# Loading the odd-numbered weight slabs of a two-block transformer kernel from GpSimd's queue instead of SyncE's

## The reference

```
first block, 2 layers:
  h = h + retention_mixer(rmsnorm(h), ...)                  # layer 0
  h = h + swiglu(rmsnorm(h), gate, up, down)                # dense, 2816 wide
  h = h + per_layer_embedding(h, ...)
  h = h + band_attention_mixer(rmsnorm(h), ...)             # layer 1
  h = h + sum over 8 experts e of gates[e] * swiglu(xn, w_gate[e], w_up[e], w_down[e])   # 3584 wide
  h = h + per_layer_embedding(h, ...)
second block, 2 layers:
  x = x + hybrid_mixer(rms_norm(x), ...)                    # stick-breaking, sparse and gated linear attention
  x = x + square(relu(rms_norm(x) @ w_up)) @ w_down         # 4096 wide
```

## Time and profile before

| | us |
|---|---|
| median of 3 runs (2742.73 to 2752.49) | 2751.07 |
| the profiled execution | 2758.43 |
| its span, from the first instruction to the last | 2756.6 |
| TensorE busy in it | 2576.8 (93%) |
| VectorE busy | 1884.1 (68%) |
| ScalarE busy | 1461.9 (53%) |
| GpSimd busy | 0.2 |

### The profile page before, as it was taken

One profiled execution on the slowest core, in us unless ns is written; L12 is line 12 of the kernel. 1 busy time (PEld: TensorE's weight loads), 2 busy tenths in 40 slices (PEclk: granted clock), 3 DMA queues, 4 the chain that ended last, 5 costly groups with the idle time before them and its releaser, 6 DMA issues.

```text
span 2756.6 us, 32701 instructions
## 1 busy us (share of the span) xinstructions
PE 2576.8 (93%) x13559; PEld 2172.2 (79%) x13559; DVE 1884.1 (68%) x1960; ACT 1461.9 (53%) x1347; POOL 0.2 (0%) x4
## 2 busy tenths in 40 slices
PE   7989999896999999999999989799989999998999
PEld 7858897865788888888888777588758988876898
DVE  7454545545788888888888787557675556767554
ACT  3434334443666766767676666455544335555442
POOL 0000000000000000000000000000000000000000
PEclk9999999967999999999999999899989999998999
DMA  7534764415899999989899977255224554522453
GB/s 225 177 107 157 208 191 160 138 61 198 302 352 343 352 342 323 368 327 370 322 370 325 359 262 269 67 157 174 77 92 155 197 170 151 171 86 88 157 187 134
DMA packets 301812, 597.59 MB, mean 217 GB/s; under 512 B 13552, under 2 KB 105952, under 8 KB 301664
## 3 DMA queue, kind: packets, MB, share of 16 engines
q1 hardware_dynamic: 301664, 595.50, 62.7%
HBM read 594.41 MB, written 1.05 MB: 216 GB/s over the span
## 4 chain that ended last, share of the span: by engine, by line
PE 83%; DVE 11%; ACT 4%; issue 2%; DMA 1%; SPq 0%; DVEq 0%; ACTq 0%
PE ps L211 81%; DVE ring_rounded L702 2%; ACT high_rounded L689 1%; DVE arena_rounded L1884 1%; PE ps L1632 1%; PE ps L1207 1%; DMA ring<-in_w_down_dense 1%; DVE arena L2369 0%; DVE h L852 0%; DVE ring_rounded L1884 0%; DVE xT L639 0%; DVE xT_rounded L645 0%; DVE arena L2499 0%; DVE arena_rounded L712 0%; ACT high_rounded L1687 0%
## 5 line engine op out<-in xcount | busy, mean ns | idle before, releaser
L211 PE MATMUL ps<-high_rounded,arena_rounded 128*128 128x512 f32 x2664 | 838.0, 396 | 24.5 <-DVE arena_rounded L712 12.4
L702 DVE TENSOR_TENSOR ring_rounded<-ring,high_rounded 128x2048 fp32r<-128x2048 f32 (+3 forms) x231 | 513.5, 2231 | 328.3 <-ACT high_rounded L689 327.3
L689 ACT ACTIVATE high_rounded<-ring 128x2048 fp32r<-128x2048 f32 (+3 forms) x231 | 430.2, 1864 | 401.0 <-PE ps L211 386.6
L211 PEld LDWEIGHTS ps<-high_rounded,arena_rounded 128*128 128x128 f32 x2664 | 500.9, 191 | 130.5 <-DVE arena_rounded L712 14.3
L211 PE MATMUL ps<-ring_rounded,arena_rounded 128*128 128x512 f32 x1000 | 396.3, 396 | 0.0
L211 PE MATMUL ps<-xT_high_rounded,high_rounded 128*128 128x256 f32 x1280 | 365.8, 286 | 25.2 <-DVE xT_rounded L645 11.2
L211 PE MATMUL ps<-xT_high_rounded,ring_rounded 128*128 128x256 f32 x1280 | 364.0, 284 | 0.0
L211 PE MATMUL ps<-xT_rounded,high_rounded 128*128 128x256 f32 x1280 | 363.8, 284 | 0.0
L211 PE MATMUL ps<-arena_rounded 128*128 128x512 f32 x864 | 339.2, 393 | 0.0
L1884 DVE TENSOR_TENSOR arena_rounded<-arena,high_rounded 128x2048 fp32r<-128x2048 f32 x131 | 297.4, 2288 | 27.4 <-ACT high_rounded L1687 27.2
L1687 ACT ACTIVATE high_rounded<-arena 128x2048 fp32r<-128x2048 f32 x131 | 251.0, 1919 | 84.6 <-PE ps L211 83.2
(11 more groups left out here) (282 smaller groups left out, 3084.3 us busy)
## 6 DMA issues: line engine op xcount, KB each, us to landing
arena<-in_w_down_moe SPq DMA_DIRECT2D x76, 1024.0 KB, 5.2
arena<-in_w_up_moe SPq DMA_DIRECT2D x72, 1024.0 KB, 5.8
arena<-in_w_gate_moe SPq DMA_DIRECT2D x68, 1024.0 KB, 5.4
ring<-in_w_in SPq DMA_DIRECT2D x50, 1024.0 KB, 5.1
ring<-in_w_gate_moe SPq DMA_DIRECT2D x44, 1024.0 KB, 5.4
ring<-in_w_up_moe SPq DMA_DIRECT2D x40, 1024.0 KB, 5.7
ring<-in_w_down_moe SPq DMA_DIRECT2D x36, 1024.0 KB, 5.3
ring<-in_w_up SPq DMA_DIRECT2D x32, 1024.0 KB, 5.4
```

What stands on the lines that cost most here:

```text
L211: return self.pe.matmul(out, lhsT, rhs, start=start, stop=stop, skip_group_check=True)
L689: act.activation(as_rounded(m, m.highs[n % HIGHS][:, 0:size]), m.slots[n % RING][:, 0:size], ACT.Copy).then_inc(m.rounded, 1)
L702: dve.tensor_tensor(as_rounded(m, slot), slot, as_rounded(m, m.highs[n % HIGHS][:, 0:size]), ALU.subtract).then_inc(m.slabs_split, 1)
```

## The change

The slabs of odd-numbered slots are loaded from GpSimd's list. `load_stream` replaces `sync_stream` and passes over the slabs of the other parity: of five ring slots, 0, 2 and 4 stay with SyncE, 1 and 3 go to GpSimd. `load_experts` does the same with the fixed experts by position (slots 0, 2, ... 12 with SyncE, 1, 3, ... 13 with GpSimd). That is 92 stream slabs and 147 expert slabs for GpSimd. The further expert items stay with SyncE altogether; since a slot's semaphore is then raised from another queue than before, odd slots of these items count on semaphores of their own (`x_landed`). Slabs 86 and 88, loaded after the experts into odd slots, are issued by GpSimd once SyncE has passed the word (`slot_free`). Sizes, buffers, waits on TensorE and all work of PE, ACT and DVE are as before.

```
-            sync_stream(sp, m, 0, RING)
+            load_stream(sp, m, 0, RING, 0)
...
+        @block.gpsimd
+        def _(pool):
+            load_stream(pool, m, 0, m.before_experts, 1)
+            load_experts(pool, m, 1)
+            load_after_experts(pool, m)
+            load_stream(pool, m, m.before_experts + RING, len(m.stream), 1)
...
-def sync_stream(sp, m, first, last):
+def load_stream(sp, m, first, last, odd):
     for n in range(first, last):
+        if n % RING % 2 != odd:
+            continue
         if n >= RING:
             sp.wait_ge(m.slabs_read, n - RING + 1)
...
-def sync_experts(sp, m):
+def load_experts(sp, m, odd):
     fixed = ExpertRun(m, 0, FIXED)
     for pos, slab in enumerate(fixed.flat):
+        if pos % 2 != odd:
+            continue
         if pos < RING:
             sp.wait_ge(m.slabs_read, fixed.places[pos][0])
-        elif pos == RING:
+        elif pos < RING + 2:
             sp.wait_ge(m.h_ready, 10)
...
-        sp.dma_start(slab.shaped(m.slots[slot]), slab.source).then_inc(m.landed[slot], 16)
+        if slot % 2:
+            sp.sem_inc(m.slot_free, 1)
+        else:
+            sp.dma_start(slab.shaped(m.slots[slot]), slab.source).then_inc(m.landed[slot], 16)
+
+
+def load_after_experts(pool, m):
+    freed = [m.before_experts + k for k in range(RING) if (m.before_experts + k) % RING % 2]
+    for k, n in enumerate(freed):
+        pool.wait_ge(m.slot_free, k + 1)
+        pool.dma_start(m.stream[n].shaped(m.slots[n % RING]), m.stream[n].source).then_inc(m.landed[n % RING], 16)
```

More of the change, by code:

```diff
@@ L451, in place @@
     m.m_landed = [sem(f"m_landed{i}") for i in range(MRING)]
+    m.x_landed = [sem(f"x_landed{i}") for i in range(MRING // 2)]
+    m.slot_free = sem("slot_free")
     m.highs = [m.high[:, i, :] for i in range(HIGHS)]
@@ L1433, in landed @@
     def landed(self, pos):
+        if not self.opening and pos % 2:
+            value = (self.first - FIXED) * LANDINGS + 16 * (pos // MRING + 1)
+            return self.m.x_landed[pos % MRING // 2], value
         return self.m.m_landed[pos % MRING], self.first * LANDINGS + 16 * (pos // MRING + 1)
@@ L1483, in sync_experts, with sync_extra_experts @@
             m.m_landed[pos % MRING], 16)
+def sync_extra_experts(sp, m):
+    fixed = ExpertRun(m, 0, FIXED)
     sp.wait_ge(m.plan_ready, 1)
@@ L1492, in sync_experts @@
             sp.dma_start(shaped_slab(slab[1], run.slot(pos)), expert_source(m.w, bass.ds(e, 1), slab)).then_inc(
-                m.m_landed[pos % MRING], 16)
+                run.landed(pos)[0], 16)
     last = sp.value_load(m.plan[0:1, ITEMS + 1:ITEMS + 2], min_val=EXPERTS - 1, max_val=ITEMS - 1)
@@ L2619, in _ @@
             sync_first_loads(sp, m)
-            sync_stream(sp, m, 0, RING)
+            load_stream(sp, m, 0, RING, 0)
             sync_tables(sp, m)
             dense = [slab.name for slab in m.stream].index("dense.up0") + RING + 8
-            sync_stream(sp, m, RING, dense)
+            load_stream(sp, m, RING, dense, 0)
             sync_embedding(sp, m, 0, 4)
             sync_bias(sp, m)
-            sync_stream(sp, m, dense, m.before_experts)
-            sync_experts(sp, m)
+            load_stream(sp, m, dense, m.before_experts, 0)
+            load_experts(sp, m, 0)
+            sync_extra_experts(sp, m)
             sync_embedding(sp, m, 1, 12)
-            sync_stream(sp, m, m.before_experts + RING, len(m.stream))
+            load_stream(sp, m, m.before_experts + RING, len(m.stream), 0)
             sync_output(sp, m, out)
+        @block.gpsimd
[4 more added lines that the diff above has]
+            load_stream(pool, m, m.before_experts + RING, len(m.stream), 1)
         @block.tensor
```

## The result

The changed kernel takes 2759.99 us (median of 18 runs, 2754.82 to 2762.95) against 2752.34 us of the kernel before in the same runs (18 runs). The ratio is 1.0028, 95% interval 1.0017 to 1.0038: 7.7 us slower, measurable, and within the 0.5% that had been called no change.

What follows compares the result with a forecast made beforehand. TensorE was taken as the bound, with loads waiting for it. The start's +2.5 and the bias loads' +1.5 gave +4.0 us on the median 2751.07, so 2755 us; own range 2742 to 2765, 8 in 10 from 2743 to 2800.

Steps and rivals of the forecast that it cites:

- Bound and reserve: Whole kernel: TensorE is the bound; slabs have 21.4 us to spare in the experts, 12.4 us in the stream.
- Step 1 and 2: Issuing: 239 issues leave SyncE, worth 0; GpSimd issues them, slabs about 3 us late within the reserve, worth 0.
- Step 3: Start: slabs 1 and 3 share the DMA engines with input and tables, delaying all work; +2.5 us, range 0 to 5.3.
- Step 4: Bias loads: slab 46 on its own queue draws bandwidth from the bias and slab 45; +1.5 us, range 0 to +2.9.
- Step 5 and 6: Hand-over after the experts costs one semaphore hop, worth 0; total supply keeps its 12% reserve, worth 0.
- A: Experts and stream: GpSimd can't issue fast enough; at 16 ns per piece +113 us, 2870; chance 0.08.
- B: Experts: GpSimd and VectorE get in each other's way; at 1.5 us per slab +96 us, 2850; chance 0.07.
- C: Experts: two queues are served worse than one; at 330 GB/s +44 us, 2798; chance 0.07.
- D: Short-width parts of the mixers: delay of 8 to 12 us makes slabs late; +20 us, with the start 2779; chance 0.10.
- E: Bias and embedding: SyncE no longer holds slabs 46 and 48 behind them; 2745 at best; chance beyond 0.5% 0.04.

Runs made afterwards that it cites:

- the first experiment: The changed kernel, but GpSimd waits until the eight gain tables have landed before issuing slabs 1 and 3; ratio 1.0007 to the kernel before.
- the second experiment: The changed kernel, but GpSimd issues slab 46 only when slab 45 has landed; ratio 1.0012 to the kernel before.
- the fifth experiment: The changed kernel, but GpSimd issues all 294 slabs of the seven fixed experts and SyncE none; ratio 1.0021 to the kernel before.
- the fourth experiment: The kernel before, but GpSimd issues the 147 expert slabs of odd position, SyncE still the whole stream; ratio 0.9998 to the kernel before.

## Why the prediction was right, step by step

- *Bound and reserve.* Right. No DMA wait of over 0.5 us has appeared except at the two places named. The 12.4 us of the stream were tested with delays of one and two slabs and hold to about 1 us. What the reckoning left out: the delay of an issue can bring it into the way of the next one.
- *Step 1 and 2, issuing.* Right, and the unknown was near the lower end. An issue takes 0.70 to 0.89 us, and the median landing of GpSimd's large stream groups is 5.4 to 6.0 us, against 4.9 to 5.4 of SyncE's, where 3 us more had been taken. In the experts both queues' loads land later than before, in 6.1 to 8.3 us instead of 5.4, well within the 21.4 us of reserve.
- *Step 3, the start.* The size was right (2.5 taken, 2.2 at the first split, 2.56 at the last table), but in part by luck, since the way to it was half right. The input was said to be late as well, by 2 to 3 us; it was late by 0.2. From 2 to 5.5 us the changed kernel sends 276 packets of SyncE's queue and none of GpSimd's, although the first of GpSimd's loads was issued at 1.24: the input had all but landed (5.89) when they began. Only what lay behind it was held up. The shares were not equal either. From 6.5 to 11 us of the changed kernel, packets, MB and share by queue:

```profile
q0 software_dynamic: 341, 1.33, 83.3%
q1 hardware_dynamic: 339, 0.25, 19.8%
```

  The queues do take turns, 341 and 339 packets, but GpSimd's carry 3.9 KB and SyncE's, with the small tables and the first slab, 0.7 KB. By bytes it is 5 to 1. The Trainium skill has this turn by packets ("DMA: Bandwidth & Descriptors", section "Queues, rings and completion order"), and the trace agrees.
- *Step 4, the bias place.* The mechanism was right, the size mis-set: 1.5 us taken, with 2.9 as the upper bound, and 4.5 us measured between the same two splits. TensorE's wait alone grew by 3.8 - 0.9 = 2.9 us, the upper bound. The bias loads ahead of 45 are in pieces of 256 bytes to 1 KB, GpSimd's packets are 4 KB. From 320 to 322 us:

```profile
q0 software_dynamic: 99, 0.41, 74.9%
q1 hardware_dynamic: 99, 0.15, 27.8%
```

  So slab 46 drew nearly three bytes for each one of SyncE's queue, the last bias load landed 17.4 us after its issue instead of 14.6, and 46 was there when ScalarE came to it, ahead of 45. The other 1.6 us are the lower clock behind the wait, which had not been thought of. It follows the long wait: with TensorE waiting 3.8 and 3.4 us (the changed kernel, the first experiment) the stretch from 333 to 339 us shows 0.72, part of it at the lower of the two levels, 1.2 GHz; with waits of 0.9 and 1.0 us (the kernel before, the second experiment) it shows 1.00.
- *Step 5 and 6.* Right: 833.83 us of 840 in the experts, 344 GB/s, the hand-over without a wait.
- *The sum.* +4.0 forecast, +7.7 measured (interval +4.7 to +10.5). The two places give 2.2 + 4.5 = 6.7 us in the profiled executions, inside the interval. The term set too low is step 4. The spans of the two executions differ by only 4.2 us because other moments gave 3.7 us back in this pair. Against the forecast of 2755 us the median of 2759.99 us is 5 us high, 3.7 us of them because the change costs more than forecast and 1.3 because of the kernel before, whose median over 18 runs is 2752.34 and not 2751.07.
- *The rivals.* A (issuing too slow) is refuted at double its load by the fifth experiment; B (VectorE and GpSimd in each other's way) by the same as a cost, with VectorE's experts' splits at 2287 ns as before, though not as a mechanism (below); C (two queues served worse) by 344 against 346 GB/s and by the fourth experiment. D and E did not occur.
- *What B had right.* Turned round, B's mechanism is in the trace. A cast of VectorE before, and the same cast after with the GpSimd issue that it falls into:

```profile
298.24 0.43 DVE L1104 CAST arena_rounded<-arena 128x512 fp32r<-128x512 f32 x1
```

```profile
296.79 0.81 DVE L1106 CAST arena_rounded<-arena 128x512 fp32r<-128x512 f32 x1
...
296.49 0.88 POOL L2793 DMA_DIRECT2D ring<-in_w_gate_dense  x1 [11.32 <-PE ps L211]
```

  Twenty of VectorE's 1960 operations take over 0.06 us longer than the same ones before, all of them during an issue of GpSimd: 4 casts, 14 tensor_scalars and 2 copies, 4.0 us together. The 247 tensor_tensors that fall into an issue take as long as before, to 0.02 us. That fits the page of the Trainium skill that the prediction drew on, "SBUF — State Buffer", which counts copies and casts among the operations in which VectorE and GpSimd shut each other out, and not a tensor_tensor. Its box tells of the other direction, GpSimd held up by VectorE; no row here shows that. In this kernel the 4.0 us cost nothing that can be measured, because such operations are few.

## What to carry to other kernels

Where the issuing queue waits for the compute engine and not the other way, a second queue has nothing to give back, and it can only let loads overtake that were needed first. Go through the few places where a load is waited for, the start above all, and ask what the new queue puts beside it. If slabs are split over two queues all the same, let the second one wait for the landing of what is needed first: two such waits took the change from 1.0028 to 0.9991. Where TensorE comes to wait longer, look at the granted clock behind the wait too: here 2.9 us of longer wait came with 1.6 us of lower clock.

## What the runs showed of the hardware that was not expected

- Loads from GpSimd go out in packets of 3.9 KB where SyncE's have 1.9 KB in this kernel. Once both queues send, they take turns by packets: 341 to 339 packets, but 1.33 to 0.25 MB, and 99 to 99, but 0.41 to 0.15 MB. A queue of large packets starves one of small ones.
- GpSimd's issue hardly depends on the number of pieces (0.70 us for 256, 0.89 us for 1024), and its landing is 0.4 to 0.7 us later than SyncE's for the same tensor of the stream.
- At equal times of issue SyncE's load goes first. In the run with one slab late GpSimd's slabs of the last MLPs need 7.7 us to landing in the median, where they need 5.4 to 6.0 otherwise, and at the start none of GpSimd's packets went out before 5.5 us. Whether the transfer in front or something in the making of the descriptors held them was not tried.
- A cast of VectorE that falls into a GpSimd issue takes 0.81 us instead of 0.43; a tensor_tensor takes as long as before.
- Behind TensorE waits of 3.8 and 3.4 us the granted clock falls for some us, here to 0.72 in a stretch of 6 us; behind waits of 0.9 and 1.0 us it does not.
